# Down products on idle PSUM banks, early split gelu tiles, and a later wait for the sub-keys

## The reference

```python
def conv_ffn(x, w_up, conv_w, w_down):
    u = x @ w_up                                  # 1024 -> 2 * 2816
    u = conv(u, conv_w, taps=3, causal, per channel)
    gate, val = jnp.split(u, 2, axis=-1)
    return (jax.nn.gelu(gate) * val) @ w_down     # 2816 -> 1024
```

```python
q = (xb @ w_query).reshape(T, 8, 2, 128)
s = jnp.einsum('thpk,hpnk->thpn', q, sub_keys)    # 16 score matrices of 128 keys
top_s, top_i = lax.top_k(s, 16)
...                                               # pairs, the best 16 of them, softmax
act = gelu(einsum('td,thkd->thk', xb, expert_u[idx]))
return einsum('thk,thkd->td', gate * act, expert_v[idx])
```

## Time and profile before

| | |
|---|---|
| median of 3 runs | 2822.88 us (2820.32 to 2832.59) |
| the profiled execution | 2819.14 us |
| its span, first to last instruction | 2817.4 us |
| TensorE busy | 2707.2 us, 96% of the span |
| VectorE, ScalarE busy | 54%, 38% |
| mean granted clock of TensorE | 0.979 |

### The profile page before, as it was taken

The page is one execution under the profiler, slowest core; times in us unless marked ns, Lnnn a source line. Parts: engine busy times, 40 slices in busy tenths (PEclk is TensorE's granted clock), DMA queues, the critical chain, the costliest instruction groups (busy, mean ns, idle before and its releaser), DMA issues.

```text
span 2817.4 us, 33396 instructions
## 1 busy us (share of the span) xinstructions
PE 2707.2 (96%) x13009; PEld 2248.5 (80%) x13009; DVE 1512.1 (54%) x2480; ACT 1077.8 (38%) x1468; POOL 202.7 (7%) x127
## 2 busy tenths in 40 slices
PE   7989998999999996899999999999999999999997
PEld 6867777888787884788888888888888888888886
DVE  4364654655534764477667565656324444444444
ACT  4344453433325435333333345555433333333332
POOL 0010000000000000000011233333100000000000
PEclk9988999999999998999999999999999999999998
DMA  5223342233232220333444454545565655566552
GB/s 194 84 67 98 113 127 90 90 92 99 90 95 80 85 74 22 118 100 97 149 141 149 124 175 180 202 179 202 198 229 192 202 200 187 186 198 205 187 187 82
DMA packets 148508, 392.11 MB, mean 139 GB/s; under 512 B 10944, under 2 KB 44752, under 8 KB 146832
## 3 DMA queue, kind: packets, MB, share of 16 engines
q1 hardware_dynamic: 94176, 274.86, 30.9%
q10 hardware_dynamic: 51904, 102.77, 10.4%
q0 software_dynamic: 2288, 12.54, 1.2%
HBM read 318.82 MB, written 71.30 MB: 138 GB/s over the span
## 4 chain that ended last, share of the span: by engine, by line
PE 92%; DVE 4%; ACT 2%; DMA 1%; issue 1%; DVEq 0%; POOL 0%; SPq 0%; ACTq 0%; POOLq 0%
PE PS L263 27%; PE PS L265 27%; PE PS L264 27%; PE PS L1915 4%; PE PS L1711 1%; PE PS L1832 1%; PE PS L1795 1%; PE PS L1782 1%; DVE WL L258 1%; PE PS L1893 1%; DMA RAW<-in_w_in 0%; PE PS L1714 0%; PE PS L407 0%; DMA A<-in_subk 0%; ACT WH L252 0%
## 5 line engine op out<-in xcount | busy, mean ns | idle before, releaser
L258 DVE TENSOR_TENSOR WL<-RAW,WH 128x1024 fp32r<-128x1024 f32 x462 | 593.8, 1287 | 807.8 <-ACT WH L252 761.3
L263 PE MATMUL PS<-HH,WH 128*128 128x512 f32 x1696 | 668.1, 394 | 14.3 <-DMA A<-in_subk 8.7
L252 ACT ACTIVATE WH<-RAW 128x1024 fp32r<-128x1024 f32 x462 | 486.0, 1053 | 461.7 <-PE PS L265 441.9
L264 PE MATMUL PS<-HL,WH 128*128 128x512 f32 x1696 | 661.0, 390 | 0.0
L265 PE MATMUL PS<-HH,WL 128*128 128x512 f32 x1696 | 660.7, 390 | 0.0
L263 PE MATMUL PS<-WH,WGH 128*128 128x512 f32 x1024 | 398.5, 389 | 0.7 <-ACT ROW L1002 0.7
L264 PE MATMUL PS<-WL,WGH 128*128 128x512 f32 x1024 | 398.3, 389 | 0.0
L265 PE MATMUL PS<-WH,WGL 128*128 128x512 f32 x1024 | 398.3, 389 | 0.0
L263 PEld LDWEIGHTS PS<-HH,WH 128*128 128x128 f32 x1696 | 319.1, 188 | 81.6 <-DMA A<-in_subk 8.9
L265 PEld LDWEIGHTS PS<-HH,WL 128*128 128x128 f32 x1696 | 318.8, 188 | 66.3
L264 PEld LDWEIGHTS PS<-HL,WH 128*128 128x128 f32 x1696 | 319.1, 188 | 63.5
(11 more groups left out here) (319 smaller groups left out, 2951.5 us busy)
## 6 DMA issues: line engine op xcount, KB each, us to landing
RAW<-in_peer_u SPq DMA_DIRECT2D x128, 512.0 KB, 3.7
RAW<-in_peer_v SPq DMA_DIRECT2D x128, 512.0 KB, 4.1
gate_matrices<-A ACTq DMA_DIRECT2D x8, 4096.0 KB, 13.0
A<-gate_matrices ACTq DMA_DIRECT2D x32, 1024.0 KB, 7.6
A<-acts ACTq DMA_DIRECT2D x32, 1024.0 KB, 11.0
RAW<-in_w_ada SPq DMA_DIRECT2D x48, 512.0 KB, 3.8
RAW<-in_ffn_up SPq DMA_DIRECT2D x44, 512.0 KB, 3.6
acts<-GATE SPq DMA_DIRECT2D x64, 256.0 KB, 2.8
```

Of the source, the lines that this page charges most:

```text
L252: nc.scalar.activation(WHr[:, slot(c), 0:w], RAW[:, slot(c), 0:w], ACT.Copy).then_inc(sem("high_done"), 1)
L258: nc.vector.tensor_tensor(WLr[:, slot(c), 0:w], RAW[:, slot(c), 0:w], WH[:, slot(c), 0:w], ALU.subtract).then_inc(sem("low_done"), 1)
L263: nc.tensor.matmul(out, L[0], R[0], start=first, stop=False)
L264: nc.tensor.matmul(out, L[0], R[1], start=False, stop=False)
```

## The change

PE's part: the barrier goes, and the first two down chunks are multiplied in two passes, token groups 2 and 3 (banks 4 to 7) and then 0 and 1 (banks 0 to 3). ACT's and DVE's part: the loop has one round fewer, the split of gelu tiles 0 to 2 stands behind it, and the last round is written out behind that. In the query stage the wait for the sub-keys moves into `score(0)`.

```diff
-        PHASE_ENDS = ["attention", "turn", "up", "states"]
+        PHASE_ENDS = ["attention", "turn", "states"]
...
+            with act.Fori(0, NF // 2 - 1) as i:
+                up_act(i)
+            act.wait_ge(sem("up_free"), 4 + 2 * 3)
+            for m in range(3):
+                nc.scalar.activation(GSHr[:, m, :], GT[:, m, :], ACT.Copy).then_inc(sem("gt_high"), 1)
+            up_act(NF // 2 - 1)
             for k in range(NF):
-                if k == 0:
-                    for m in range(3):
-                        nc.scalar.activation(GSHr[:, m, :], GT[:, m, :], ACT.Copy).then_inc(sem("gt_high"), 1)
...
                 if k + 3 < NF:
                     act.wait_ge(sem("chunk_used"), c)
+                    act.wait_ge(sem("up_free"), 4 + 2 * (k + 4))
...
+            with dve.Fori(0, NF // 2 - 1) as i:
+                up_dve(i)
+            for m in range(3):
+                dve.wait_ge(sem("gt_high"), m + 1)
+                nc.vector.tensor_tensor(GSLr[:, m, :], GT[:, m, :], GSH[:, m, :], ALU.subtract)\
+                    .then_inc(sem("gt_low"), 1)
+            up_dve(NF // 2 - 1)
...
-            barrier(pe, "up")
-            for k in range(NF - 2):
+
+            for rows in ((2, 3), (0, 1)):
+                for k in range(2):
+                    c = (FIRST["down"] + k, 0, 0)
+                    if rows[0] == 2:
+                        pe.wait_ge(sem("low_done"), number(c, 1))
+                        pe.wait_ge(sem("gt_low"), k + 1)
+                    elif k == 0:
+                        pe.wait_ge(sem("up_free"), 4 + 2 * NF)
+                    for t in rows:
+                        ts = slice(t * P, (t + 1) * P)
+                        for h in range(2):
+                            hs = slice(h * 512, (h + 1) * 512)
+                            last = mm3(PS[:, 2 * t + h, :], (GSHr[:, k, ts], GSLr[:, k, ts]),
+                                       (WHr[:, slot(c), hs], WLr[:, slot(c), hs]), k == 0, False)
+                    if rows[0] == 0:
+                        last.then_inc(sem("chunk_used"), 1)
+            for k in range(2, NF - 2):
                 pe.wait_ge(sem("gt_low"), k + 1)
...
-            pe.wait_ge(sem("subkeys_landed"), 16)
...
             def score(n):
                 pe.wait_ge(sem("query_stored"), n + 1)
+                if n == 0:
+                    pe.wait_ge(sem("subkeys_landed"), 16)
```

More of the change, by code:

```diff
@@ L887, in _, with up_act @@
             cu = FIRST["up"]
-            with act.Fori(0, NF // 2) as i:
+            def up_act(i):
                 for j in range(4):
-                    split_high(act, (cu + j + LEAD, i, 4))
+                    split_high(act, (cu + j + LEAD, i, 4) if not isinstance(i, int) else (cu + 4 * i + j + LEAD, 0, 0))
                     act.wait_ge(sem("chunk_used"), i * 4 + (cu + j + 1))
@@ L898, in _ @@
                             .then_inc(sem("up_gelu"), 1)
-            barrier(act, "up")
+            with act.Fori(0, NF // 2 - 1) as i:
[4 more added lines that the diff above has]
+            up_act(NF // 2 - 1)
             for k in range(NF):
-                if k == 0:
-                    for m in range(3):
-                        nc.scalar.activation(GSHr[:, m, :], GT[:, m, :], ACT.Copy).then_inc(sem("gt_high"), 1)
                 c = FIRST["down"] + k
@@ L1279, in _, with up_dve @@
             cu = FIRST["up"]
-            with dve.Fori(0, NF // 2) as i:
+            def up_dve(i):
                 for j in range(4):
-                    split_low(dve, (cu + j + LEAD, i, 4))
+                    split_low(dve, (cu + j + LEAD, i, 4) if not isinstance(i, int) else (cu + 4 * i + j + LEAD, 0, 0))
                     dve.wait_ge(sem("up_tap"), i * 4 + (j + 1))
@@ L1293, in _ @@
                             .then_inc(sem("up_free"), 2)
-            barrier(dve, "up")
-            for k in range(NF):
[L1296 to L1300, removed]
+            with dve.Fori(0, NF // 2 - 1) as i:
[5 more added lines that the diff above has]
+            up_dve(NF // 2 - 1)
+            for k in range(NF):
                 c = FIRST["down"] + k
@@ L1813, in _ @@
                     mm_t(pe, (cu + j, i, 4), PS[:, j, :])
-            barrier(pe, "up")
-            for k in range(NF - 2):
+            for rows in ((2, 3), (0, 1)):
[15 more added lines that the diff above has]
+            for k in range(2, NF - 2):
                 pe.wait_ge(sem("gt_low"), k + 1)
-                mm_n1(pe, (FIRST["down"] + k, 0, 0), (GSHr[:, k % 4, :], GSLr[:, k % 4, :]), k == 0, False)
+                mm_n1(pe, (FIRST["down"] + k, 0, 0), (GSHr[:, k % 4, :], GSLr[:, k % 4, :]), False, False)
             pe.wait_ge(sem("gt_low"), NF)
```

## The result

The changed kernel took 2809.8 us in the median of 5 executions (2807.78 to 2810.76), the kernel before 2828.49 (5 executions, 2820.32 to 2832.59): ratio 0.9941, 95% interval 0.9923 to 0.9960. A second comparison with 10 and 33 executions gave 0.9952 (0.9936 to 0.9968), 2811.39 against 2823.7. So the change gains 0.5%, 12 to 14 us.

A forecast was written before the change was run, and what follows sets the result against it. TensorE, busy 96% of the span, was taken as the bound; gains of 6.8 us (down stage) and 4.4 us (queries) sum to 11.2, taking the 2822.88 median to 2811.7, put at 2811.5 us, range 2806 to 2819.

The forecast's parts named there:

- Which waits: TensorE's waits for the sub-keys' transfer (8.7 us) and the first gelu low half (5.2 us) would both leave its list.
- Part A: Start of the down stage: barrier gone, early tile splits, two passes; gain 6.8 us, 5.4 of idle and 1.4 of lower clock.
- The step that no row showed: How TensorE leaves the up loop with products right behind it; cost taken as zero, bounded above by 5.24 us.
- That rival: Leaving the up loop costs TensorE what the idle hid, or the last gelu tile comes late; 2818.5 us, chance 0.10.
- The slack ahead of bank 0: Down stage's second pass: last gelu tile ready at 750.41, TensorE there at 752.06; 1.65 us slack, wait costed at nothing.
- The cover of the moved work: End of the up stage: the early copies and halves delay up chunk 43's split, hidden by 9 us of slack.
- Part B: Start of the queries: sub-keys' wait moved to the first score; second query starts 4.4 us earlier, 2.0 at worst.
- The pitch of the tiles: Turned tiles pace query 0 at 1.31 us each, with bursts of three products taking 0.68 us.
- The price of a low clock in the bursts: Rival at query 0's bursts: low clock costs up to 2.4 us (0.6 last tile, 1.8 queries behind); 2814 us, chance 0.10.
- a clock of 0.50 at query 0: Sign named in advance: a granted clock of 0.50 at query 0 would show the prediction wrong.
- The sum: Whole kernel: 6.8 + 4.4 = 11.2 us gained, 0.40%, giving 2811.5 us; main case's chance 0.66.
- The bound of 0.5%: A measurement tells about 0.5% (14.1 us) from no change; chances 0.83 the same, 0.14 faster, 0.03 slower.

The follow-up runs named there:

- second pair of profiles: The kernel before and the changed kernel, each unchanged, profiled again beside the follow-up runs; ratios to before 0.9992 and 0.9952.
- A alone: Changed kernel with the sub-keys' wait back ahead of the queries, so only the up-to-down stage edits remain; ratio to before 0.9984 (0.9969 to 0.9999).
- B alone: Kernel before with only the sub-keys' wait moved to the first score; ratio to before 0.9981 (0.9966 to 0.9996).

## Why the prediction was right

- **Which waits.** Both went, and no other took their place except that for the turned tiles, as said.
- **Part A.** Forecast 6.8, measured 17.92 - 11.10 = 6.82 in the first pair of profiles and 17.94 - 11.11 = 6.83 in the second. The step that no row showed, how TensorE leaves its loop, costs nothing: 0.22 to 0.23 us from the last up product to the first down product, in five profiles. That rival falls, and with it the one that the Trainium skill's "Instruction fetch mechanics" in "Runtime: NRT & Kernel Launch" stood beside.
- **The slack ahead of bank 0** was worked out as 1.65 us and is 2.2. The last gelu tile is ready 3.46 us after the start of the last up product, not 4.02. The prediction missed this. All kernels with the last round written out for ScalarE and VectorE have it; that the loop's register instructions are what took the time is likely, and no run takes them away alone.
- **The cover of the moved work.** Chunk 43's low half ended at 730.4, and TensorE wanted it at 740, 9.6 us later. The forecast was 9.
- **Part B.** Forecast 4.4, measured 4.36 in the first pair and 5.13 in the second. The term was sized from one execution. How many products run at the lower clock behind the long idle differs, seven to eleven after the first, and the changed kernel has no such stretch, so B's mean over the three profiles with this idle is nearer 4.9. The pitch of the tiles was read as 1.31 us, from the end of a low half and the start of a product. From low half to low half it is 1.33 (1170.45 to 1179.77, seven steps), which changes nothing in the sum.
- **The price of a low clock in the bursts** was put at up to 2.4 us and was 0 in the one profile that had it. The 0.6 us for the last tile and 1.8 behind it are for a low stretch at the end of the bursts; it lay in the middle, under the pitch of the tiles, and what one at the end costs no run shows. The prediction also named a clock of 0.50 at query 0 as a sign that it was wrong. That sign came, in this profile, and meant nothing.
- **The sum** was 11.2, 0.40%. The two distances say 11.2 to 12.0, the better comparison 13.6 with 9.0 to 18.1 as its interval. The prediction of 2811.5 stands against 2809.8 and 2811.39. That it fits so closely is partly luck: its base, the median of three runs, happened to lie in the lower group, as did both medians of the changed kernel.
- **The bound of 0.5%.** The step that the runs scatter by some 2 us was wrong. They scatter by 10, in two groups. By them the first comparison came out at 0.59%, beyond the bound to which most of the chance was given, and the second at 0.48%.

The first two profiles differ by 10.6 us in span for reasons that partly cancel. The kernel after is 746.39 - 745.17 = 1.2 us ahead already at the last up product, which the change does not touch. From there to the start of the turn's last low half it is 1186.01 - 746.39 = 439.62 us before and 1179.77 - 745.17 = 434.60 after, only 5.0 less, though part A gave 6.8. Nothing of the change is given back in between. In the second pair of profiles the same stretch took 441.41 and 434.59 us, which is the whole 6.8, so the 1.8 are scatter of the first profile. Most of them stand behind TensorE's long wait at the end of the second block's recurrence. In the first profile of the kernel before, the clock was back at 1.00 within 4.4 us of TensorE's start there (1123.63 to 1128), in the second only after 6.2 (1134.79 to 1141). Such stretches are why a difference of spans is no measure of a change of this size, and a distance at the place is one.

## What to carry to other kernels

Ask of each wait which instruction behind it really reads what it waits for, and of each stage's first products which banks are free already. As long as the rest of an idle stretch still lets the clock fall, removing a part gives no more than its length (1.2 us for 1.5, 0.6 for 0.6 here); the last part gives more (5.1 us for 3.3). Once a transfer is off the path, look for what is late next: 8.7 us of wait were worth 4.4 to 5.2, because the turned tiles came at their own pace.

## What the runs showed of the hardware

**Two groups of times.** The kernel before gave 2821 to 2824 us in most of its executions and some 2832 in the others, and each of its variants has the same two groups, 9 to 11 us apart: 2811 and 2821 for the changed kernel, 2815 and 2826 for A alone, 2818 and 2827 for B alone. The profiles that fell in the upper group have their extra time in the first block's attention. The window from 200 to 300 us, in a profile of each group:

```profile
200.00:300.00 100.00, 94.81 (x472) 72.01 (x470) 55.16 (x109) 43.81 (x90) 0.00 (x0) 0.85 0.38 115
```

```profile
200.00:300.00 100.00, 96.58 (x422) 73.34 (x420) 48.48 (x96) 38.61 (x79) 0.00 (x0) 0.73 0.32 100
```

The mean granted clock there is 0.85 in the one and 0.73 in the other, TensorE busy in both. All twelve profiles fall this way: 0.82 to 0.85 in seven, 0.73 in the other five. The up stage then ends later (last up product at 757.29 against 745.17). The first five executions of the changed kernel were all in the lower group, and three of the five of the kernel before took 2828 to 2833, which made the first comparison too kind. Within a group, the changed kernel is 12.4 us (lower, 2823.3 to 2810.9) and 11.8 us (upper, 2832.5 to 2820.7) faster, close to the 11.2 to 12.0 of the two distances. Why an execution falls in one or the other group was not tried.

**A clock that falls late.** In the kernel without the passes, behind 3.1 us of idle, the clock was still 1.00 in the idle and in TensorE's first products, and fell 1.5 us after the work had begun again. In the kernel before, with 5.24 us of idle, it fell near the end of the idle (0.71 at 751 to 752). What a short idle costs can stand behind it in the timeline, not in it.
